# Swapping one parameter tile and two operand tiles in the SBUF plan of a three-block transformer kernel

## The reference

```
x = x + 0.5 * swiglu(norm(x), ffn1_w_in, ffn1_w_out)     # 1024 -> 2 x 2816 -> 1024
x = x + mixer(norm(x)) @ w_out                           # LRU or convolution, attention, memory attention
x = x + 0.5 * swiglu(norm(x), ffn2_w_in, ffn2_w_out)

def swiglu(x, w_in, w_out):
    a, b = jnp.split(x @ w_in, 2, axis=-1)
    return (jax.nn.silu(a) * b) @ w_out
```

## Time and profile before

| what | value |
|---|---|
| median of 3 runs | 1862.5 us (1861.96 to 1866.23) |
| profiled execution, its own time | 1861.96 us |
| span of its profile | 1860.2 us |
| PE busy | 1832.6 us (99%) |
| PEld busy | 1678.5 us (90%) |
| DVE busy | 1059.7 us (57%) |
| ACT busy | 918.9 us (49%) |
| DMA | mean 177 GB/s |

### The profile page before, as it was taken

One profiled execution on the slowest core, in us unless ns is written; L12 is line 12 of the kernel. 1 busy time (PEld: TensorE's weight loads), 2 busy tenths in 40 slices (PEclk: granted clock), 3 DMA queues, 4 the chain that ended last, 5 costly groups with the idle time before them and its releaser, 6 DMA issues.

```text
span 1860.2 us, 33328 instructions
## 1 busy us (share of the span) xinstructions
PE 1832.6 (99%) x13114; PEld 1678.5 (90%) x13114; DVE 1059.7 (57%) x1413; ACT 918.9 (49%) x1200; POOL 45.2 (2%) x66
## 2 busy tenths in 40 slices
PE   8999999999999999999999999999999999999998
PEld 8999877999999999898898999899999887889997
DVE  5544777554555455655576544555474655575554
ACT  5344566434444445576555444444454675645343
POOL 0000220000000000000000000000000000000000
PEclk9999999999999999999999999999999999999999
DMA  8555423655465555452254554555555442345552
GB/s 313 196 182 194 178 92 114 222 184 203 167 238 201 186 176 204 165 198 92 91 180 176 200 184 173 207 205 200 187 186 192 159 161 93 134 170 200 184 196 97
DMA packets 47856, 329.19 MB, mean 177 GB/s; under 512 B 5392, under 2 KB 5648, under 8 KB 9616
## 3 DMA queue, kind: packets, MB, share of 16 engines
q1 hardware_dynamic: 44496, 316.84, 47.4%
q10 hardware_dynamic: 3264, 11.03, 1.8%
HBM read 326.80 MB, written 1.05 MB: 176 GB/s over the span
## 4 chain that ended last, share of the span: by engine, by line
issue 82%; PE 14%; POOL 1%; DVE 1%; ACT 1%; DMA 0%; DVEq 0%; POOLq 0%; ACTq 0%
PE work L1477 3%; PE work L1479 3%; PE work L1478 3%; POOL rstd L539 1%; PE acc L1477 1%; PE acc L1478 1%; PE acc L1479 1%; DVE lo L987 0%; DMA pre<-pre 0%; PE acc L1674 0%; PE acc L1570 0%; ACT hi L588 0%; PE acc L1694 0%; ACT squared L608 0%; PE acc L1683 0%
## 5 line engine op out<-in xcount | busy, mean ns | idle before, releaser
L987 DVE TENSOR_TENSOR lo<-raw,hi 128x2048 fp32r<-128x2048 f32 x280 | 640.3, 2291 | 476.8 <-ACT hi L588 476.5
L1477 PE MATMUL work<-xT_hi,hi 128*128 128x256 f32 x2752 | 770.8, 280 | 1.4 <-DVE lo L987 1.1
L1479 PE MATMUL work<-xT_hi,lo 128*128 128x256 f32 x2752 | 763.6, 277 | 0.0
L1478 PE MATMUL work<-xT_lo,hi 128*128 128x256 f32 x2752 | 763.6, 277 | 0.0
L588 ACT ACTIVATE hi<-raw 128x2048 fp32r<-128x2048 f32 x280 | 534.0, 1911 | 233.9 <-PE work L1479 188.1
L1477 PEld LDWEIGHTS work<-xT_hi,hi 128*128 128x128 f32 x2752 | 516.9, 188 | 17.9 <-issue 12.0
L1478 PEld LDWEIGHTS work<-xT_lo,hi 128*128 128x128 f32 x2752 | 517.0, 188 | 2.5
L1479 PEld LDWEIGHTS work<-xT_hi,lo 128*128 128x128 f32 x2752 | 518.9, 189 | 0.0
L1479 PE MATMUL acc<-hi,hT_lo 128*128 128x512 f32 x480 | 188.7, 393 | 0.0
L1478 PE MATMUL acc<-lo,hT_hi 128*128 128x512 f32 x480 | 188.2, 392 | 0.0
L1477 PE MATMUL acc<-hi,hT_hi 128*128 128x512 f32 x480 | 187.1, 390 | 0.0
(11 more groups left out here) (261 smaller groups left out, 2016.0 us busy)
## 6 DMA issues: line engine op xcount, KB each, us to landing
raw<-stream SPq DMA_DIRECT2D x298, 1024.0 KB, 4.8
pre<-pre ACTq DMA_DIRECT2D x7, 512.0 KB, 5.7
mem_in<-mem ACTq DMA_DIRECT2D x3, 1024.0 KB, 6.1
post<-post ACTq DMA_DIRECT2D x6, 512.0 KB, 3.8
x<-x SPq DMA_DIRECT2D x2, 512.0 KB, 4.9
pre<-pre SPq DMA_DIRECT2D x2, 512.0 KB, 3.5
out<-x SPq DMA_DIRECT2D x4, 256.0 KB, 2.0
alibi<-alibi ACTq DMA_DIRECT2D x1, 768.0 KB, 14.4
```

The source lines that it names most:

```text
L987: nc.vector.tensor_tensor(lo[:, s, :], raw[:, s, :], hi[:, s, :].bitcast(F32), ALU.subtract).then_inc(lo_ready, 1)
L1477: nc.tensor.matmul(dst, a_hi, b_hi, start=start, stop=False)
L1478: nc.tensor.matmul(dst, a_hi, b_lo, start=False, stop=False)
L1479: return nc.tensor.matmul(dst, a_lo, b_hi, start=False, stop=stop)
```

## The change

`params` is taken after `xT_hi` and `xT_lo` instead of ahead of them. No instruction, wait, loop or transfer is added, removed or moved; every tile after `params` keeps its place, since the three rooms together are as large as before.

```diff
         xs = place("xs", [P, TT, D], r_scaled)
         heads1 = place("heads1", [P, TT, 16, HD], r_scaled)
         rot = place("rot", [P, TT, 16, HD], r_scaled)
-        params = new("params", [P, max(B1P_N, LP_N)])
         xT_hi = new("xT_hi", [P, KD, T], F32R)
         xT_lo = new("xT_lo", [P, KD, T], F32R)
+        params = new("params", [P, max(B1P_N, LP_N)])
         pre = new("pre", [P, D])
         post = new("post", [P, D])
```

## The result

The changed kernel takes 1910.66 us (median of 4 runs, 1907.2 to 1911.33) against 1863.63 us for the kernel before: a ratio of 1.0239, 95% interval 1.0226 to 1.0251. It is 2.4% slower, outside the range of 1853 to 1884 us, and by more than the dearest rival (1888 us). The profiled execution has a span of 1908.0 us, 47.8 us more than before.

The account below looks back on a forecast made before the run. PE's number of matmuls times their start-to-start distance was taken as the bound. 1861.96 + 0 + 0 + 0 = 1861.96 us; the shown runs' median is 0.5 us more, so 1862.5 us, range 1853 to 1884 us.

Parts of the forecast that it names:

- What bounds the kernel: PE, busy 99% of the span: its number of matmuls times the distance from one start to the next sets the time.
- Two cadences, and the entry decides between them: Matmuls with `xT` start 117.9 or 113.3 ns apart; how PE enters a stretch sets which, until the next disturbance.
- The terms for `params` and for the writes of `xT`: ACT and DVE reading `params` and writing `xT` at new addresses: 0 each, `params` 2.3 us if the cover were gone.
- The third term: 8256 PE matmuls reading `xT` at a new offset against the stationary chunks: 0 us, bounded by all fast and all slow.
- a shared offset forces neither the slow nor the fast cadence: Conclusion from key compression (117.8 and 113.3 ns across differing offsets) and gates (mean 278 ns), used for the 0 us.
- The gates: Rows called nearest to the state after the change, stationary tile at `xT`'s offset within 512 bytes: mean 278 ns, between both cadences.
- The reasoning from layer 0 against layer 1: Convolution's 112 triples, same addresses, at 281 ns in layer 0 and 276 in layer 1: address cannot be the whole cause.
- The rival of the slow cadence: Shared offset makes nearly all stretches enter the slow cadence: 25.8 us more, 1888 us; chance 0.30 for two or more further FFNs.
- The sign I had given for a wrong prediction: The same cadence in every stretch would show that it follows the operands' offset rather than the way a stretch is entered.
- The rival of the fast cadence everywhere: With operands on a common grid the slow stretches turn fast: 8.2 us less, 1854.3 us; chance 0.26.
- one below 113.3 ns: Cadence of 256-column matmuls falls toward 106.7 ns: at most 54 us won, 1808 us; chance 0.02.
- The Trainium skill's rule: PE's read ports for moving operand and LDWEIGHTS are independent, so the term for reading `xT` is exactly 0 at any address.

Follow-up runs that it names:

- hT64n: hT64 plus one extra 32-column matmul, result unused, ahead of each of the 60 later chunks: 1867.18 us, ratio 1.0001 to the kernel before.
- x192n: x192 plus one extra 32-column matmul, result unused, ahead of each of the 60 later chunks: 1897.31 us, ratio 1.0158 to the kernel before.
- x192: Changed kernel with `xT_hi` and `xT_lo` shifted to 192 bytes past a multiple of 512, `params` still behind: 1863.94 us, ratio 0.9993 to the kernel before.
- ring320: Changed kernel with the ring (`raw`, `hi`, `lo`) moved up by 320 bytes, `xT` at the same offset within 512: 1868.47 us, ratio 1.0018 to the kernel before.
- lo64: Changed kernel with only the stationary `lo` moved up by 64 bytes: 1900.64 us, ratio 1.0188 to the kernel before.
- split: Changed kernel with `xT_hi` 192 bytes past a multiple of 512 and only `xT_lo` on one: 1893.7 us, ratio 1.0130 to the kernel before.
- hT64: x192 with every tile from `r_qT` on, `hT` and `hT_last` among them, moved by 64 bytes: 1880.42 us, ratio 1.0085 to the kernel before.
- x256: Changed kernel with `xT` shifted to 256 bytes past a multiple of 512: 1908.7 us, ratio 1.0235 to the kernel before.
- x128: Changed kernel with `xT` shifted to 128 bytes past a multiple of 512: 1910.22 us, ratio 1.0243 to the kernel before.
- x160: Changed kernel with `xT` shifted to 160 bytes past a multiple of 512: 1897.96 us, ratio 1.0158 to the kernel before.

## Why the prediction was wrong, point by point

**What bounds the kernel** was right. PE's number of matmuls times their distance sets the end; 48 us more on PE became 48 us more in the span, and none of it was hidden.

**Two cadences, and the entry decides between them** was right for the good offset and is now shown there, by hT64n and x192n. It can account for why layer 0 and layer 1 differ at equal addresses: in x192 it is the other way round, with 113.5 ns in layer 0's convolution stretch and 117.6 in layer 1's. That a cadence "then holds until the next disturbance" was too strong, as the key compression shows below.

**The terms for `params` and for the writes of `xT`** were right at 0: its readers kept 484 and 476 ns, and x192, with `params` in its new place, is at 0.9993.

**The third term, "PE reads `xT` at another address", is the step that failed**, in its value and in its bounds. I took 0 and bounded it by all fast and all slow, -8.2 to +25.8 us; it measured +44 us and 2 us more at the `br` matmuls. The sentence at fault is that "a shared offset forces neither the slow nor the fast cadence". It was drawn from two kinds of rows, and both were misread.

In the key compression the stationary operand moves on by 120 bytes at every pair. The cadence there changes from 117.8 to 113.3 ns in the middle of the stretch, with no wait and no other instruction in between, so no new entry explains it; what changes is the address. The trace of the kernel before has more of this. The first two rows are the same five pairs in layer 1, the last two the same five in layer 0's second compression, whose `cmp` tiles stand 5760 bytes further on (128 past a multiple of 256); 15 distances lie between the rows of each pair:

```profile
1481.57 0.28 PE L1477 MATMUL work<-hi,cmp_hi 128*30 128x256 f32 x1
...
1483.27 0.28 PE L1477 MATMUL work<-hi,cmp_hi 128*30 128x256 f32 x1
...
818.85 0.28 PE L1477 MATMUL work<-hi,cmp_hi 128*30 128x256 f32 x1
...
820.62 0.28 PE L1477 MATMUL work<-hi,cmp_hi 128*30 128x256 f32 x1
```

1.70 us again in layer 1, but 1.77 us in the second compression, 118.0 ns each. The second compression could differ in more than that, its PSUM bank for one; but in ring320, where the ring moved by 320 bytes and `cmp` kept its offset within 512 bytes, the five pairs of the first compression take 1.76 us. So the fast cadence returned at the same pairs, whatever the layer, and went away when the distance between the operands changed: these rows were a sign that the address acts, and the prediction took them for a sign that it doesn't. They were no bound either, since a load of 30 columns at offsets that change every three matmuls doesn't show what one constant offset costs a full load.

The gates have 24 columns, and only the first of their 8 tiles stands on the common offset, the next being 96 bytes on; I had called them the nearest rows, and they were the nearest only in name.

What the runs showed in its place is a mean distance for each offset modulo 256 bytes, from 114.3 to 119.8 ns, with the kernel before at the one good value of those tried, and 120.0 ns in the changed kernel's chunks where the bound had stopped at 117.8. All the large tiles behind `params` in the kernel before stand 192 past the ring's offset, so its trace could not show the size of this cost.

**The reasoning from layer 0 against layer 1** went one step too far. Equal addresses with different cadences prove that something beside the address acts. They do not prove that the address doesn't; here both do. At 192 and 448 (and once at 64) there are two cadences and the entry chooses; at 0, 128 and 256 no chunk of a network has either of them.

**The rival of the slow cadence** had the right sign and the right mechanism, "moving and stationary reads now begin on the same offset", and 0.30 of chance; its price was too small because it took 117.8 ns for the worst that there was. The sign I had given for a wrong prediction, the same cadence in every stretch, is what came: 282 to 284 ns in all. The rival of the fast cadence everywhere and that of one below 113.3 ns did not come in any run: no 42 distances in a row with `xT` moving have a mean below 113.3 ns in any of the traces.

**The Trainium skill's rule**, in "SBUF — State Buffer", section "Who interferes with whom", that PE's two read ports are independent and PE never waits for anyone, gave 0 at any address. x192 and the changed kernel differ in nothing but the place of `xT` and padding, and by 47 us in time; ring320 shows that it is the relation of the two operands. The measurement decides: the time of PE's matmuls does depend on where its two operands lie to one another, whether or not the ports are what waits.

What stays open: what lies inside PE or SBUF that has this period of 256 bytes. That the two reads meet in some shared part is an argument from x192, ring320 and lo64, not a thing that any row shows. Nor is there a rule yet for which entry leads to which cadence, and it is not known how much of the losses at 64 bytes, in split and in lo64 another entry would win back.

## What to carry to other kernels

Where PE is busy all the time with many matmuls, read the distance from start to start in the timeline, per stage, and compare it across stages that do the same work; the busy share won't show it. The distance between the addresses of the moving operand and of the stationary operands loaded beside it is then a tuning parameter, worth up to 6% of the distance from start to start and 2.5% of the time in this kernel, of period 256 bytes here; scan it with padding in steps of 32 or 64 bytes, and scan it again after any edit of the SBUF plan, since one tile's size shifts all that follow. And when a term is bounded by neighbouring rows, ask whether they share what makes the case, here a full load and an offset that stays, and whether they change where only the address does.

## What the runs showed of the hardware that was not expected

- Matmuls in float32r with 256 moving columns start 113.3 to 120.0 ns apart in long stretches at the 2.4 GHz level, with no wait in between, depending on the distance between operands modulo 256 bytes and on the entry. The worst of the offsets tried costs 120.0 / 113.3, 5.9%, over the best place's fast cadence. With 512 columns the means are 226.5 to 233.5 ns.
- At one offset two cadences can hold chunk after chunk, and one matmul of 32 columns ahead of a chunk switches between them, in both directions: 13 us won in hT64n against hT64, 33 us lost in x192n against x192. A change in the addresses of the matmuls ahead does it as well: 16 us lost in hT64 against x192.
- With one of three moving operands badly placed (split), all three distances rose, to 117.7, 119.6 and 116.6 ns, which together is the slow cadence.
- Loads (LDWEIGHTS) beside L1477 have a mean of 191 ns in the changed kernel and in x256 in place of 188, but 189 in x128 and 188 in x160, which are nearly as slow: their duration is no sure sign.
